# Head rounds of a hybrid attention and mLSTM layer: one quarter of a projection unit goes from slot 0 to slot 14, and three pieces of order with it

## The chip, the cores and the metric

The kernel runs on one core of a Trainium2 chip. The metric is the device time of one execution in microseconds; smaller is better. TensorE (PE) multiplies, PEld is its weight load, VectorE is DVE, ScalarE is ACT, GpSimd is POOL and SyncE is SP.

## The reference

One layer in float32, for 1024 tokens of width 1024. Two mixers read the same normalised input: a differential attention with 8 heads and an mLSTM with 8 heads. Their outputs are gated, projected and added, and a feed-forward part follows.

```python
proj = jnp.einsum('bsd,de->bse', rms_norm(h, norm_mix_w[l]), w_in[l])
(da_q, da_k, da_v, ml_q, ml_k, ml_v, ml_i, ml_f, ml_o, gate_pre) = jnp.split(proj, split_idx, axis=-1)
oa = diff_attention(qa, ka, va, lam, cos, sin)       # softmax(q0 k0) v - lam softmax(q1 k1) v, causal
hm = mlstm_chunkwise(qm, km, vm, i_pre, f_pre)
merged = g[:, :, 0] * (rms_norm(oa) @ w_proj_a) + g[:, :, 1] * ((sigmoid(ml_o) * rms_norm(hm)) @ w_proj_b)
h = h + merged @ w_out
h = h + (relu(rms_norm(h) @ w_ff1) ** 2) @ w_ff2
```

## The kernel before

Products in full precision are made of three matmuls on rounded parts: high times high, high times low, low times high. Each operand is therefore split by one engine into a high part (a copy on ACT) and a low part (a subtraction on DVE or POOL).

The projection of one head is six blocks of 128 columns, and each block is two **units** of 512 tokens. So a head has 12 units, called unit 0 to unit 11 here. Unit k accumulates in the PSUM bank `gp0` if k is even and in `gp1` if it is odd. It has 24 matmuls and is cut into four **quarters** of six. ACT copies a finished bank to `ev0` or `ev1` (the **eviction**, `evac`, L1041), and SP stores it to DRAM. There are only two banks, so on PE a unit begins with a wait (`gp_free`, in `unit`) for the eviction of the unit two before it.

A **head round** works on two heads at once. It makes the 12 units of head h, and between them it does the attention and the mLSTM of head h-1. It has 16 slots. `QUARTERS` gives the number of quarters that PE runs in each slot, and behind them stands the slot's piece of the other head's work, `attend(h, s)`. There are seven head rounds, for h = 1 to 7; a last round of another form (units of the gates, by `GATE_UNITS_AT`) carries the work of head 7.

What `attend` does on PE in the slots that matter: slot 0 transposes v into the banks `tr` and `ob` (L777), slot 2 does the same for the mLSTM's v, slots 3 to 10 make the scores of query tiles 0 to 7 (L799 to L803), slots 4 to 12 transpose the weights of a tile and multiply them by v (L863, L838, L849, L850), slots 11 to 13 hold the mLSTM's products, slot 13 also transposes the attention's output (L890), and slot 15 transposes the mLSTM's output (`hm`, L897), for which DVE must have scaled `nd` (L1625).

Every engine runs its own list in program order. ACT's list for a slot is written by `head_round` in the scalar block: first the split of a weight block into its high part (`split_hi`, L1036) if a block begins in this slot, then the evictions of `ENDS_AT[s][:-1]`, then `attend`, then the eviction of the last unit that ends in this slot. `ENDS_AT[s]` holds the units whose last quarter lies in slot s; it is worked out from `QUARTERS`. In slots 3 to 10 ACT's `attend` ends with the two exponentials of a tile (L1158), which wait for the scores on PE and their maximum on DVE. In slot 0 the eviction stands inside `attend`, behind the copies of k. DVE makes the low parts of k, q and v in slot 0 (L1503 to L1521), the maxima (L1542), the bias `nb` (L1544) and the low parts of the weights (L1526). POOL makes the low parts of the weight blocks (L1910) and one product of the mLSTM in slot 8 (L1934).

Of the kernel before, what the change touches and what calls it, by code (L numbers as in the profile page):

```python
# [26 lines left out]
TT = S // P  # L27
# [52 lines left out]

SLOTS = 16

QUARTERS = (4, 4, 5, 0, 3, 2, 3, 3, 4, 4, 4, 4, 2, 2, 4, 0)


def part_slots(quarters):

    at = [s for s, n in enumerate(quarters) for _ in range(n)]
    starts = [[k for k in range(2 * HB) if at[4 * k] == s] for s in range(SLOTS)]
    ends = [[k for k in range(2 * HB) if at[4 * k + 3] == s] for s in range(SLOTS)]  # L90
    return at, starts, ends


QUARTER_AT, STARTS_AT, ENDS_AT = part_slots(QUARTERS)

# [4 lines left out]
def wait(eng, sem, value):  # L100

    if isinstance(value, int) and value <= 0:
        return
    eng.wait_ge(sem, value)


def tr_index(i, second):

    return i + max(0, i - 4) + (1 if second else 0)
# [22 lines left out]
def build(nc, x, x_rows, positions, norm_mix_w, in_blocks, in_if, columns, da_lambda,  # L132
# [13 lines left out]
    with ExitStack() as ctx:  # L146
        def sb(name, shape, dt=F32, scope=ctx):
            return scope.enter_context(nc.sbuf_tensor(name, shape, dt))
# [69 lines left out]
        with heads, ExitStack() as sc:  # L218
            qraw = sb("qraw", [P, S], F32, sc)
            kraw = sb("kraw", [P, S], F32, sc)  # L220
            qs = sb("qs", [P, 2, S], F32R, sc)
# [809 lines left out]
        def _(act):  # L1031
            def split_hi(n, half_n, slot):

                act.wait_ge(w_loaded[slot], 16 * half_n + 16)
                wait(act, gemm_done, 2 * n - 2)
                act.activation(wh[slot][:], raw[slot][:], ACT.Copy).then_inc(w_hi, 1)  # L1036

            def evac(n, half):
                wait(act, st[half], 16 * n)
                act.wait_ge(gemm_done, 2 * n + half + 1)  # L1040
                act.activation(ev[half][:], gp[half][:], ACT.Copy).then_inc(gp_free, 1)  # L1041
                act.wait_ge(gp_free, 2 * n + half + 1)
                act.sem_inc(ev_ready[half], 1)
# [54 lines left out]
            def units_of_round(h, k):  # L1098
                if k % 2 == 0:
                    b = k // 2  # L1100
                    split_hi(h * HB + b + 1, h * (HB // 2) + (b + 1) // 2, (b + 1) % 2)
# [3 lines left out]
                evac(k // 2, k % 2)  # L1105
                prologue_step(k)

            def attend(h, s, evac_units):
                def v_part(i):
                    act.wait_ge(vtr, 4 * h + 1 + i)  # L1110
                    src = (tr, ob)[i][:].rearrange("p (t n) -> p t n", t=4)
                    act.activation(vs[:, 4 * i:4 * i + 4, 0:DV], src, ACT.Copy).then_inc(v_hi, 1)

                if s == 0:
                    for c, (x_, to) in enumerate(((kraw, ka), (qraw, qs))):
                        act.wait_ge(roped, 2 * h + c + 1)
                        act.activation(to[0:DK, 0, :], x_[0:DK, :], ACT.Copy).then_inc(qk_hi, 1)
                        act.activation(to[DK:P, 1, :], x_[DK:P, :], ACT.Copy).then_inc(qk_hi, 1)
                        if c == 0:
                            act.activation(kb[DK:P, 0, :], x_[0:DK, :], ACT.Copy).then_inc(qk_hi, 1)  # L1120
                            act.activation(kb[0:DK, 1, :], x_[DK:P, :], ACT.Copy).then_inc(qk_hi, 1)
                            evac_units()
                    v_part(0)
                    v_part(1)
                if s == 2:
                    for i in range(2):
                        act.wait_ge(vtr, 4 * h + 3 + i)
# [4 lines left out]
                def high(i, second):  # L1132
                    act.wait_ge(tr_done, 12 * h + tr_index(i, second) + 1)
                    if not second:
                        wait(act, pv_done, TT * h + i)
                    j0, j1 = (4, i + 1) if second else (0, min(4, i + 1))
                    act.activation(ath[:, j0:j1, :], tr[:, 0:(j1 - j0) * P].rearrange("p (j n) -> p j n", n=P),
                                   ACT.Copy).then_inc(a_hi, 1)

                i = s - 5  # L1140
                if 0 <= i < TT:
                    if i >= 4:
                        high(i, True)
                    act.wait_ge(pv_done, TT * h + i + 1)
                    wait(act, sso_done, TT * h + i)
                    act.activation(otmp[:], ob[:, DV:2 * DV], ACT.Copy).then_inc(o_right, 1)
                if 0 <= s - 4 < TT:
                    high(s - 4, False)
                i = s - 5
# [3 lines left out]
                i = s - 3  # L1153
# [44 lines left out]

            def head_round(h, att):
                for s in range(SLOTS):  # L1200
                    for k in STARTS_AT[s]:
                        if k % 2 == 0:
                            units_of_round(h, k)
                    for k in ENDS_AT[s][:-1]:
                        evac(h * HB + k // 2, k % 2)

                    def evac_units():
                        for k in ENDS_AT[s][-1:]:
                            evac(h * HB + k // 2, k % 2)

                    attend(att, s, evac_units)
                    if s:
                        evac_units()

            head_round(1, 0)
            with act.Fori(2, NH) as h:
                head_round(h, h - 1)
            for s in range(SLOTS):
                for k in GATE_UNITS_AT[s]:
                    n = N_GATE + k // 2  # L1220
                    if k % 2 == 0:
                        split_hi(n + 1, (n + 1) // 2, (n + 1) % 2)
                for k in GATE_UNITS_AT[s]:
                    evac(N_GATE + k // 2, k % 2)
                attend(NH - 1, s, lambda: None)
# [17 lines left out]
            for j in range(2 * KT):  # L1243
# [7 lines left out]
                else:  # L1251
                    for i in range(2):
                        k = j - KT
# [151 lines left out]
        def _(dve):  # L1405
# [92 lines left out]
            def attend(h, s):  # L1498
                if s == 0:
                    chain.start(h * DVE_HEAD)  # L1500
                    def low_parts(c, x_, to):
                        dve.wait_ge(qk_hi, 6 * h + 4 * c + 2)
                        dve.tensor_tensor(to[DK:P, 0, :], x_[0:DK, :], to[0:DK, 0, :].bitcast(F32), ALU.subtract).then_inc(qk_lo, 1)  # L1503
                        dve.tensor_tensor(to[0:DK, 1, :], x_[DK:P, :], to[DK:P, 1, :].bitcast(F32), ALU.subtract).then_inc(qk_lo, 1)


                    for x_, turned, s_in in ((kraw, kqs, k_in), (qraw, sg, q_in)):
                        dve.wait_ge(s_in, 16 * 5 * (h + 1))
                        dve.tensor_tensor(turned[:], turned[:], sinT[:], ALU.mult)
                        chain.link(dve.tensor_tensor(x_[:], x_[:], cosT[:], ALU.mult))  # L1510
                        if x_ is qraw:
                            low_parts(0, kraw, ka)
                        dve.tensor_tensor(x_[:], x_[:], turned[:], ALU.add).then_inc(roped, 1)
                    dve.wait_ge(qk_hi, 6 * h + 4)
                    dve.tensor_tensor(kb[0:DK, 0, :], kraw[0:DK, :], kb[DK:P, 0, :].bitcast(F32), ALU.subtract).then_inc(qk_lo, 1)
                    dve.tensor_tensor(kb[DK:P, 1, :], kraw[DK:P, :], kb[0:DK, 1, :].bitcast(F32), ALU.subtract).then_inc(qk_lo, 1)
                    low_parts(1, qraw, qs)
                    for i in range(2):
                        dve.wait_ge(v_hi, 2 * h + i + 1)
                        src = (tr, ob)[i][:].rearrange("p (t n) -> p t n", t=4)  # L1520
                        dve.tensor_tensor(vs[:, 4 * i:4 * i + 4, DV:2 * DV], src, vs[:, 4 * i:4 * i + 4, 0:DV].bitcast(F32),  # L1521
                                          ALU.subtract).then_inc(v_lo, 1)
                def low(i, second):
                    dve.wait_ge(a_hi, 12 * h + tr_index(i, second) + 1)
                    j0, j1 = (4, i + 1) if second else (0, min(4, i + 1))
                    dve.tensor_tensor(atl[:, j0:j1, :], tr[:, 0:(j1 - j0) * P].rearrange("p (j n) -> p j n", n=P),  # L1526
                                      ath[:, j0:j1, :].bitcast(F32), ALU.subtract).then_inc(a_lo, 1)

                i = s - 5
# [6 lines left out]
                if 0 <= s - 4 < TT:  # L1536
                    low(s - 4, False)
                i = s - 3
# [97 lines left out]
            for s in range(SLOTS):  # L1636
                attend(0, s)
            with dve.Fori(1, NH) as h:
                for s in range(SLOTS):
                    attend(h, s)  # L1640
# [5 lines left out]
            for j in range(2 * KT):  # L1646
                n = N_PA + j
                for i in range(2):
                    k = j % KT
# [432 lines left out]
```

## Time and profile before

| | |
|---|---|
| median of 3 runs | 1958.7 us (1956.92 to 1960.9) |
| the profiled execution, its own time | 1959.85 us |
| its span, first to last instruction | 1957.6 us |
| PE busy | 1906.0 us, 97% |
| one head round (526.08 to 630.44 us) | 104.36 us |
| granted TensorE clock, mean | 0.997 |

A view of waits has a row for each pair of an engine's line and the work that released it: total, times, longest. A timeline row is the start, the duration, the engine, the line and the tiles (written from read), and in brackets how long the engine had been idle and what ended that. A PE duration reaches past the start of the next matmul, because they overlap; the distance of two starts is what one costs.

### The profile page before, as it was taken

What the parts mean: (1) busy time and instruction counts of PE and PEld (TensorE: products, weight loads), DVE (VectorE), ACT (ScalarE), POOL (GpSimd) and SP (SyncE); (2) the same over time, 40 slices, a digit from 0 to 9 for tenths busy, and PEclk for the clock granted to TensorE, in tenths of its full rate; (3) what the DMA queues carried; (4) which work ended last, traced back from release to release, by engine and by line L of the source; (5) the groups of instructions that cost most, each with busy time, mean ns of one, the idle gap of its engine ahead of it and who ended that gap; (6) DMA issues with size and microseconds to landing.
All of it is one profiled execution on the core that took longest, in us unless ns stands there. A gap on an engine that the chain in (4) does not pass through costs nothing. (4 is left out here: it accounts for less than half of the span.)

```text
span 1957.6 us, 25826 instructions
## 1 busy us (share of the span) xinstructions
PE 1906.0 (97%) x9314; PEld 1592.5 (81%) x9314; DVE 1188.0 (61%) x1538; ACT 958.3 (49%) x1618; POOL 365.8 (19%) x203
## 2 busy tenths in 40 slices
PE   6999999999999999999999999999999999999998
PEld 5788888888888888878888888878887888888886
DVE  6755666666665757543422122488777777789774
ACT  4355565656564655544434223226485665433341
POOL 1221212112121121212223444440000000121002
PEclk9999999999999999999999999999999999999999
DMA  4251514242423333252244434457576686564412
GB/s 168 89 172 55 178 55 157 74 150 86 148 88 123 107 101 134 72 173 67 81 158 144 156 119 159 174 192 269 201 273 235 211 295 223 187 235 146 155 65 86
DMA packets 91872, 291.77 MB, mean 149 GB/s; under 512 B 10872, under 2 KB 11640, under 8 KB 80784
## 3 DMA queue, kind: packets, MB, share of 16 engines
q1 hardware_dynamic: 89488, 282.31, 41.9%
q10 hardware_dynamic: 2304, 8.39, 1.1%
q8 instruction: 51, 0.84, 0.2%
q14 instruction: 29, 0.24, 0.0%
HBM read 203.56 MB, written 87.10 MB: 148 GB/s over the span
## 5 line engine op out<-in xcount | busy, mean ns | idle before, releaser
L708 PE MATMUL gp<-r1h,w_hi 128*128 128x512 f32 x1152 | 454.6, 395 | 2.2 <-POOL w_lo L1910 2.2
L710 PE MATMUL gp<-r1h,w_lo 128*128 128x512 f32 x1152 | 450.1, 391 | 0.0
L709 PE MATMUL gp<-r1l,w_hi 128*128 128x512 f32 x1152 | 449.5, 390 | 0.0
L1910 POOL TENSOR_TENSOR w_lo<-w_raw,w_hi 128x1024 fp32r<-128x1024 f32 x87 | 218.1, 2507 | 857.3 <-ACT w_hi L1036 857.3
L710 PEld LDWEIGHTS gp<-r1h,w_lo 128*128 128x128 f32 x1152 | 216.6, 188 | 46.4
L708 PEld LDWEIGHTS gp<-r1h,w_hi 128*128 128x128 f32 x1152 | 216.7, 188 | 45.4 <-POOL w_lo L1910 2.6
L709 PEld LDWEIGHTS gp<-r1l,w_hi 128*128 128x128 f32 x1152 | 216.9, 188 | 41.8
L956 PE MATMUL scores<-xh,qh 128*128 128x512 f32 x512 | 200.3, 391 | 3.2 <-ACT res L1309 2.3
L958 PE MATMUL scores<-xl,qh 128*128 128x512 f32 x512 | 199.2, 389 | 0.0
L960 PE MATMUL scores<-xh,ql 128*128 128x512 f32 x512 | 199.2, 389 | 0.0
L1158 ACT ACTIVATE pr<-scores,nb 128x256 f32<-128x256 f32 (+7 forms) x128 | 93.8, 738 | 117.8 <-DVE nb L1544 116.2
L1041 ACT ACTIVATE ev<-gp 128x512 f32<-128x512 f32 x128 | 75.7, 591 | 135.1 <-PE gp L710 129.0
L1722 DVE TENSOR_TENSOR xl<-xraw,xh 128x2048 fp32r<-128x2048 f32 x54 | 132.2, 2447 | 0.0
L1269 ACT ACTIVATE qh<-rq 128x2048 fp32r<-128x2048 f32 x32 | 61.2, 1913 | 117.4 <-DVE rq L1751 71.3
L956 PEld LDWEIGHTS scores<-xh,qh 128*128 128x128 f32 x512 | 96.1, 188 | 25.7 <-ACT res L1309 4.2
L1036 ACT ACTIVATE w_hi<-w_raw 128x1024 fp32r<-128x1024 f32 x88 | 93.0, 1057 | 44.0 <-PE gp L710 21.0
L960 PEld LDWEIGHTS scores<-xh,ql 128*128 128x128 f32 x512 | 96.1, 188 | 20.2
L958 PEld LDWEIGHTS scores<-xl,qh 128*128 128x128 f32 x512 | 96.1, 188 | 20.0 <-issue 0.2
L1542 DVE TENSOR_REDUCE mx<-scores 128x1 f32<-128x256 f32 (+7 forms) x128 | 91.2, 749 | 30.2 <-PE scores L803 29.7
L1281 ACT ACTIVATE xh<-xraw 128x2048 fp32r<-128x2048 f32 x54 | 102.8, 1903 | 9.9 <-DMA xraw<-xo_d 9.8
L1992 POOL TENSOR_TENSOR hb<-hb,sqacc 128x1024 f32<-128x1024 f32 x8 | 24.6, 3074 | 434.4 <-DMA hb<-h_d 434.4
L1726 DVE TENSOR_TENSOR ql<-rq,qh 128x2048 fp32r<-128x2048 f32 x32 | 74.3, 2322 | 46.3 <-ACT qh L1269 46.3
(327 smaller groups left out, 3698.2 us busy)
## 6 DMA issues: line engine op xcount, KB each, us to landing
xraw<-xo_d SPq DMA_DIRECT2D x54, 1024.0 KB, 5.4
w_raw<-in_in_blocks SPq DMA_DIRECT2D x64, 512.0 KB, 3.7
proj_d<-ev SPq DMA_DIRECT2D x128, 256.0 KB, 2.0
rq<-in_ff_quarters SPq DMA_DIRECT2D x32, 1024.0 KB, 8.0
xo_d<-res SPq DMA_DIRECT2D x78, 256.0 KB, 3.3
xo_d<-ring SPq DMA_DIRECT2D x60, 256.0 KB, 3.0
pr<-proj_d SPq DMA_DIRECT2D x16, 512.0 KB, 4.6
gt<-proj_d SPq DMA_DIRECT2D x32, 256.0 KB, 3.5
```

The lines of the kernel that those rows point to most:

```text
L708: pe.matmul(gp[half][:], wh[slot][:, k, :], mh[:, k, t], start=(k == 0), stop=False)
L709: pe.matmul(gp[half][:], wh[slot][:, k, :], ml[:, k, t], start=False, stop=False)
L710: mm = pe.matmul(gp[half][:], wl[slot][:, k, :], mh[:, k, t], start=False, stop=(k == KT - 1))
L956: pe.matmul(bank, qh[s % 3][:, k, cols], xh[s % 3][:, k, :], start=first and k == 0, stop=False, skip_group_check=True)
L958: pe.matmul(bank, qh[s % 3][:, k, cols], xl[s % 3][:, k, :], start=False, stop=False, skip_group_check=True)
L960: mm = pe.matmul(bank, ql[s % 3][:, k, cols], xh[s % 3][:, k, :], start=False, stop=(k == UN - 1), skip_group_check=True)
L1036: act.activation(wh[slot][:], raw[slot][:], ACT.Copy).then_inc(w_hi, 1)
L1158: act.activation(pr[:, c, 0:(i + 1) * P], sp_[:, c, 0:(i + 1) * P], ACT.Exp, bias=nb[:, c:c + 1], scale=SCALE, accum_out=rs[:, i, c:c + 1] ...
L1281: act.activation(xh[s % 3][:], xraw[(s + 1) % 2][:], ACT.Copy).then_inc(p_hi, 1)
L1542: m = dve.tensor_reduce(mx[:, c:c + 1], sp_[:, c, 0:(i + 1) * P], AX_X, ALU.max)
L1722: dve.tensor_tensor(xl[s % 3][:], xraw[(s + 1) % 2][:], xh[s % 3][:].bitcast(F32), ALU.subtract).then_inc(p_lo, 1)
L1910: pool.tensor_tensor(wl[slot][:], raw[slot][:], wh[slot][:].bitcast(F32), ALU.subtract).then_inc(w_split, 1)
```

## The change

`QUARTERS` gives slot 0 three quarters in place of four, and slot 14 five in place of four. As the quarters are dealt to the slots in order, each slot from 1 to 14 that has quarters now begins with the one that had been the last of the slot with quarters before it. `STARTS_AT` and `ENDS_AT` follow from the table. ACT makes the high parts of v ahead of those of q, and DVE the low parts of v ahead of those of q. From slot 9 on ACT splits a weight block behind the copy of the late columns of a tile's weights (`high(i, True)`).

```diff
-QUARTERS = (4, 4, 5, 0, 3, 2, 3, 3, 4, 4, 4, 4, 2, 2, 4, 0)
+QUARTERS = (3, 4, 5, 0, 3, 2, 3, 3, 4, 4, 4, 4, 2, 2, 5, 0)
...
-            def attend(h, s, evac_units):
+            def attend(h, s, evac_units, splits=None):
...
                             evac_units()
-                    v_part(0)
-                    v_part(1)
+                            v_part(0)
+                            v_part(1)
...
                 i = s - 5
+                if 4 <= i < TT:
+                    high(i, True)
+                if splits:
+                    splits()
                 if 0 <= i < TT:
-                    if i >= 4:
-                        high(i, True)
...
-                    for k in STARTS_AT[s]:
-                        if k % 2 == 0:
-                            units_of_round(h, k)
+                    def splits():
+                        for k in STARTS_AT[s]:
+                            if k % 2 == 0:
+                                units_of_round(h, k)
+
+                    if s < 9:
+                        splits()
...
-                    attend(att, s, evac_units)
+                    attend(att, s, evac_units, splits if s >= 9 else None)
...
-                    low_parts(1, qraw, qs)
                     for i in range(2):
                         dve.wait_ge(v_hi, 2 * h + i + 1)
...
+                    low_parts(1, qraw, qs)
```

Worked out from the table, the slot in which each unit ends (and behind whose `attend` it is evicted) is:

| unit | 0 | 1 | 2 | 3 | 4 | 5 | 6 | 7 | 8 | 9 | 10 | 11 |
|---|---|---|---|---|---|---|---|---|---|---|---|---|
| before | 0 | 1 | 2 | 4 | 6 | 7 | 8 | 9 | 10 | 11 | 13 | 14 |
| now | 1 | 2 | 2 | 5 | 6 | 8 | 9 | 10 | 11 | 12 | 14 | 14 |

The first place is PE at the end of slot 8 and the start of slot 9 in the first head round, ahead of unit 7 (bank `gp1`). Before:

```order
L799 MATMUL scores<-mask,identr 128x256
L801 MATMUL scores<-ka,qs 128x256
L803 MATMUL scores<-kb,qs 128x256
L708 MATMUL gp1<-r1h,w_hi1 128x512 [waits gp_free]
L709 MATMUL gp1<-r1l,w_hi1 128x512
L710 MATMUL gp1<-r1h,w_lo1 128x512
```

The same place in the changed kernel:

```order
L799 MATMUL scores<-mask,identr 128x256
L801 MATMUL scores<-ka,qs 128x256
L803 MATMUL scores<-kb,qs 128x256
L708 MATMUL gp0<-r1h,w_hi1 128x512
L709 MATMUL gp0<-r1l,w_hi1 128x512
L710 MATMUL gp0<-r1h,w_lo1 128x512
L708 MATMUL gp0<-r1h,w_hi1 128x512
L709 MATMUL gp0<-r1l,w_hi1 128x512
L710 MATMUL gp0<-r1h,w_lo1 128x512
L708 MATMUL gp1<-r1h,w_hi1 128x512 [waits gp_free]
```

One quarter of unit 6 now stands between the scores of tile 5 and the wait of unit 7.

The second place is ACT from the second sigmoid of slot 7 (`osig`) to the eviction behind the exponentials of tile 5 (`pr`, 128x768) in slot 8. Before:

```order
L1171 ACTIVATE osig<-osig 128x1024 [waits o_in]
L1041 ACTIVATE ev1<-gp1 128x512 [waits gemm_done,proj_stored1]
L1036 ACTIVATE w_hi0<-w_raw0 128x1024 [waits gp_free,gemm_done,w_loaded0]
L1146 ACTIVATE otmp<-ob 128x128 [waits sso_done,pv_done]
L1137 ACTIVATE ath<-tr 128x512 [waits pv_done,tr_done]
L1152 ACTIVATE otmp,sso<-oo 128x128 [waits o_add]
L1158 ACT_TABLE_LOAD [waits a_done]
L1158 ACTIVATE pr,rs<-scores,nb 128x768 [waits nb_ready]
L1158 ACTIVATE pr,rs<-scores,nb 128x768
L1041 ACTIVATE ev0<-gp0 128x512 [waits gemm_done,proj_stored0]
```

In the changed kernel:

```order
L1173 ACTIVATE osig<-osig 128x1024 [waits o_in]
L1036 ACTIVATE w_hi0<-w_raw0 128x1024 [waits gemm_done,w_loaded0]
L1148 ACTIVATE otmp<-ob 128x128 [waits sso_done,pv_done]
L1137 ACTIVATE ath<-tr 128x512 [waits pv_done,tr_done]
L1154 ACTIVATE otmp,sso<-oo 128x128 [waits o_add]
L1160 ACT_TABLE_LOAD [waits a_done]
L1160 ACTIVATE pr,rs<-scores,nb 128x768 [waits nb_ready]
L1160 ACTIVATE pr,rs<-scores,nb 128x768
L1041 ACTIVATE ev1<-gp1 128x512 [waits gemm_done,proj_stored1]
```

The eviction of `gp1` (unit 5), which stood ahead of the split, now stands behind the exponentials.

The third place is ACT in slots 0 to 2 of the first head round, as a piece of the difference:

```order
 L1120 ACTIVATE kb<-kraw 64x1024
 L1121 ACTIVATE kb<-kraw 64x1024
-L1041 ACTIVATE ev0<-gp0 128x512 [waits gemm_done,proj_stored0]
-L1117 ACTIVATE qs<-qraw 64x1024 [waits gp_free,roped]
-L1118 ACTIVATE qs<-qraw 64x1024
 L1112 ACTIVATE vs<-tr 128x4x128 [waits vtr]
 L1112 ACTIVATE vs<-ob 128x4x128 [waits vtr]
-L1041 ACTIVATE ev1<-gp1 128x512 [waits gemm_done,proj_stored1]
+L1117 ACTIVATE qs<-qraw 64x1024 [waits roped]
+L1118 ACTIVATE qs<-qraw 64x1024
+L1041 ACTIVATE ev0<-gp0 128x512 [waits gemm_done,proj_stored0]
 L1036 ACTIVATE w_hi0<-w_raw0 128x1024 [waits gp_free,gemm_done,w_loaded0]
```

The eviction of unit 0 moves from between k and q to behind v and q.

## Rows read from the trace of the kernel before

**Rows 1.** Page: the busy time of each engine.

```profile
PE 1906.0 (97%) x9314; PEld 1592.5 (81%) x9314; DVE 1188.0 (61%) x1538; ACT 958.3 (49%) x1618; POOL 365.8 (19%) x203
```

**Rows 2.** Waits of PE: line, waited for, us in total, times, longest.

```profile
PE tr L897 <- DVE nd L1625: 6.0, 7, 0.9
PE ob L849 <- DVE atl L1526: 3.8, 7, 0.6
PE tr L777 <- DVE vs L1521: 3.2, 6, 0.5
PE scores L882 <- DVE cst L1597: 2.7, 7, 0.4
```

**Rows 3.** Timeline of PE, slots 15 to 2 of one round change.

```profile
526.08 0.66 PE L897 MATMUL tr<-ident,nd 128*128 128x128 f32 x4 [0.87 <-DVE nd L1625]
...
533.28 0.48 PE L708 MATMUL gp<-r1h,w_hi 128*128 128x512 f32 x1
...
546.37 0.66 PE L777 MATMUL tr<-ident,pr 128*128 128x128 f32 x4 [0.54 <-DVE vs L1521]
```

**Rows 4.** Timeline of all engines, the same round, slots 0 and 1.

```profile
538.11 0.57 ACT L1041 ACTIVATE ev<-gp 128x512 f32<-128x512 f32 x1
...
538.73 0.19 PEld L708 LDWEIGHTS gp<-r1h,w_hi 128*128 128x128 f32 x1 [0.16 <-ACT ev L1041]
538.76 1.23 DVE L1513 TENSOR_TENSOR qraw<-qraw,sg 128x1024 f32<-128x1024 f32 x1
...
542.19 0.60 ACT L1112 ACTIVATE vs<-tr 128x512 fp32r<-128x512 f32 x1
```

**Rows 5.** Timeline of PE: first projection matmuls of slots 9 to 12.

```profile
579.18 0.39 PE L708 MATMUL gp<-r1h,w_hi 128*128 128x512 f32 x1
...
580.56 0.39 PE L708 MATMUL gp<-r1h,w_hi 128*128 128x512 f32 x1
...
588.50 0.48 PE L708 MATMUL gp<-r1h,w_hi 128*128 128x512 f32 x1
...
598.97 0.48 PE L708 MATMUL gp<-r1h,w_hi 128*128 128x512 f32 x1
...
609.57 0.48 PE L708 MATMUL gp<-r1h,w_hi 128*128 128x512 f32 x1
```

**Rows 6.** Timeline of ACT: the evictions that close slots 8 to 11.

```profile
585.76 0.59 ACT L1041 ACTIVATE ev<-gp 128x512 f32<-128x512 f32 x1
...
595.42 0.57 ACT L1041 ACTIVATE ev<-gp 128x512 f32<-128x512 f32 x1
...
605.27 0.59 ACT L1041 ACTIVATE ev<-gp 128x512 f32<-128x512 f32 x1
...
610.64 0.59 ACT L1041 ACTIVATE ev<-gp 128x512 f32<-128x512 f32 x1
```

**Rows 7.** Timeline of DVE in slot 8: the bias of tile 5.

```profile
582.23 1.72 DVE L1544 TENSOR_SCALAR nb<-mx 128x2 f32<-128x2 f32 x1
```

**Rows 8.** Timeline of POOL in slot 8.

```profile
581.53 2.39 POOL L1934 TENSOR_TENSOR kqs<-kqs,sg 128x1024 f32<-128x1024 f32 x1
```

**Rows 9.** Timeline of ACT and of PE, slot 0 of the first round.

```profile
120.06 1.06 ACT L1118 ACTIVATE qs<-qraw 64x1024 fp32r<-64x1024 f32 x1
...
116.93 0.48 PE L708 MATMUL gp<-r1h,w_hi 128*128 128x512 f32 x1
```

**Rows 10.** Timeline of PE near the program's start.

```profile
24.60 0.79 PE L734 MATMUL scores<-r1h,wifh 128*128 128x512 f32 x1 [2.60 <-DVE r1l L1426]
...
30.31 0.39 PE L734 MATMUL scores<-r1h,wifh 128*128 128x512 f32 x1
```

**Rows 11.** Timeline of PE, first units of the gates.

```profile
865.18 0.50 PE L708 MATMUL gp<-r1h,w_hi 128*128 128x512 f32 x1 [2.22 <-POOL w_lo L1910]
...
866.76 0.63 PE L708 MATMUL gp<-r1h,w_hi 128*128 128x512 f32 x1
```

**Rows 12.** That stretch: us, five engines' busy time, granted clock, DMA share, GB/s.

```profile
862.00:874.00 12.00, 9.78 (x41) 7.65 (x40) 2.20 (x3) 3.56 (x7) 5.68 (x6) 0.86 0.63 203
```

## The prediction

> **What bounds the kernel now.** I read the page first: PE is busy for 1906.0 us, 97% of the span [rows 1], and no other engine passes 61%. So only what PE waits for can be won or lost, and the waits of PE are the second view. Four rows of it lie in the head rounds: 6.0 us for the scaled `nd` in slot 15, 3.8 us for the low parts of late columns in slot 10, 3.2 us for v's low parts in slot 2, and 2.7 us for the mLSTM's state in slot 13 [rows 2]. That is 15.7 us over seven rounds, all that an edit of these rounds could win from waits. The third view is the timeline of one round, engine beside engine, to see how much time lies between the end of each eviction on ACT and the matmul that needs its bank. There the margin is thin. In slot 0 the eviction of unit 0 starts at 538.11 and takes 0.57 us, and the weight load of unit 2 at 538.73 has already waited 0.16 us for it [rows 4].
>
> **What the change adds: evictions that come too late.** PE has two banks, so unit k+2 waits for the eviction of unit k. Moving one quarter out of slot 0 makes most units end one quarter inside the next slot. Their eviction follows that slot's `attend`, so on ACT it moves back by a whole slot, while on PE the start of unit k+2 moves back by one quarter only. A quarter costs 580.56 - 579.18 = 1.38 us [rows 5]. I take the places in turn, with the round of the rows as the measure; the position of an eviction within its slot is that of the row of before that stood at the same place in ACT's list.
>
> *Slot 9, unit 7 waits for unit 5.* PE is behind the scores of tile 5 at 579.18 and has one quarter to run, until 580.56 [rows 5]. The eviction of unit 5 stood at the end of slot 7, ahead of the split of slot 8; now it stands behind the exponentials of slot 8, where that of unit 6 stood, at 585.76 for 0.59 us [rows 6]. ACT comes there a little sooner: the eviction, 0.57 us, and the wait for its own semaphore no longer stand ahead of the split. The bias of tile 5 took 1.72 us and ended at 583.95, with POOL's product ending at 583.92 beside it [rows 7, 8]; POOL's list follows the split, so both end about 0.75 us sooner. The eviction ends at 585.76 + 0.59 - 0.75 = 585.6. Wait: 5.05 us.
>
> *Slot 10, unit 8 waits for unit 6.* PE: 588.50 + 1.38 = 589.88. ACT: 595.42 + 0.57 = 595.99 [rows 5, 6]. Both shift together, since the exponentials of tile 6 wait for scores that PE makes after its last wait. Wait: 6.1 us.
>
> *Slot 11, unit 9 waits for unit 7.* PE: 598.97 + 1.38 = 600.35. ACT: 605.27 + 0.59 = 605.86 [rows 5, 6]. Wait: 5.5 us.
>
> *Slot 12, unit 10 waits for unit 8.* PE: 609.57 + 1.38 = 610.95; ACT: 610.64 + 0.59 = 611.23 [rows 5, 6]. There are no exponentials in slot 11. Wait: 0.3 us.
>
> *Slot 2, unit 2 waits for unit 0.* The transposes of slot 15 start at 526.08 after a wait of 0.87 us [rows 3]. With one more quarter ahead of them PE comes 1.38 us later: the wait is gone and they start 1.38 - 0.87 = 0.5 us later, and DVE's work behind them too. Behind the transposes of v PE resumes at 533.28 + 0.5 - 1.38 = 532.4 [rows 3], runs five quarters (one of unit 0, four of unit 1), and stands before unit 2 at 539.3. ACT now evicts unit 0 behind v and q. The copies of q wait for q's rotation, which ends at 538.76 + 1.23 + 0.5 = 540.5, so v's copies are done in that time, and the second copy of q gives way where it did, half a microsecond later: 542.19 + 0.5 = 542.7 [rows 4]. The eviction ends at 543.3. Wait: 4.0 us. In the first head round this does not happen: PE resumes at 116.93, stands before unit 2 some 5.5 us later, at 122.4, and the second copy of q is done at 120.06 + 1.06 = 121.1 [rows 9], so the eviction ends at 121.7.
>
> At slots 4 to 8 I cost the change at nothing: unit 3 is evicted behind slot 5 and unit 5 needs its bank only in slot 7; unit 4 stays in slot 6. Two quarters or more and an `attend` cover each. Unit 9's eviction falls behind slot 12, and unit 11 needs it in slot 14. Its store is late on SP and delays the loads of the next k by some 4 us; the rotation that reads them is a slot and more away.
>
> **What it removes.** Of the row for slot 15, 6.0 us, all goes. Of the row for slot 2, 3.2 us, all goes, since PE now reaches slot 2 at 543.3 + 5.5 = 548.8, while DVE is done with v and q half a microsecond later than in the row, at 546.37 + 0.5 = 546.9 [rows 3]. Of the row for slot 10, 3.8 us, all goes: the late columns are copied ahead of the split, and that split is what held them. The row for slot 13 stays, because the chain to it starts in slot 12 behind PE's own work.
>
> **The sum.** For six round changes: 4.0 added, 0.54 and the 0.16 at unit 2 taken away, 3.3 each, 20 us. For seven rounds: 5.05 + 6.1 + 5.5 + 0.3 = 16.95 added and 0.54 taken away, 16.4 each, 115 us. Less the 6.0 us of slot 15. That is 129 us.
>
> **The clock adds to each wait.** PE will stand still 21 times for over 5 us, and six times for 4 us. The trace has one wait of this kind with a fall behind it: PE stood for 2.22 us before 865.18, and from 866.76 on its 128x512 matmuls take 0.63 us in place of 0.39 [rows 11], the levels of 1.2 and 2.4 GHz. The granted clock of these 12 us is 0.86 [rows 12], which is 12 x 0.14 / 0.5 = 3.4 us at the low level, and half of that, 1.7 us, is lost. At the program's start the low level lasted from 24.60, behind 2.60 us of idling, to 30.31 [rows 10]; 5.7 us of work at half rate lose 2.8 us, the dearest case that the trace has. So the cost of one long wait lies between nothing, if a fall happens to end while PE still stands, and 2.8 us. I take 1.6 us for each of the 27, next to the row from the middle of the program: 43 us; the bounds are 0 and 76 us.
> The Trainium skill, TensorE: Matmul & The Clock Gate, "HAM oscillation — how this bites in real kernels", says that an idle stretch between bursts puts the array back to half rate, so that in a loop every burst starts cold, and that the moment varies from run to run. The trace agrees as far as it goes, with 1.7 us at its single case. Left out of the sum, the rule would mean 2088 us in place of 2131.
>
> The profiled execution took 1959.85 us, so its like is 1959.85 + 129 + 43 = 2132. It stood 1.15 us above the median; the predicted median is 2131 us, 172 us slower. About 0.2% is what a measurement of this kernel tells from no change.
>
> **The rivals.**
> *The low level lasts as at the start, behind nearly every wait.* Speaks for it: the waits come four to a round, three of them with some 9 us between, and they are two to three times as long as the two in the rows. Against: the wait of 2.22 us lost 1.7 us only. At 2.8 us each: 1959.85 + 129 + 76 - 1 = 2164; from 2150 up. Chance 0.15.
> *The clock hardly falls.* For it: the fall ends while PE still stands, so that a long wait may cost less than a short one. Against: a wait of 2.22 us was enough. 2088 with no fall at all; up to 2112 here. Chance 0.2.
> *The evictions hold nobody, and the waits that the change aims at go.* The mechanism is that ACT would reach the copy of a bank before PE needs it; it decides if the time from the scores to the end of the exponentials is under one quarter, 1.38 us. The rows say 6 to 7 us (579.18 to 585.76, 588.50 to 595.42) [rows 5, 6], so I see no way but an error in my reading of who waits for which unit. Then six times 0.54, the slot 10 row and half of the slot 15 row go (DVE starts 0.5 us later, which reaches slot 3): some 10 us, 1949. Chance 0.03; some 0.01 for the case that it comes out within 0.2%.
> *The waits are shorter than summed.* If the row positions of ACT are off by 1 us at each of the 27 waits, 27 us less than the forecast: 2104, inside the range.
>
> **How the numbers follow.** Forecast 0.61, with its own range of 2112 to 2150. The range of 8 in 10 takes in about half of either clock rival: 2100 to 2160. Faster 0.03, same 0.01, slower 0.96.
>
> **What would show it.** In the waits of PE a row `gp L708 <- ACT ev L1041` of some 27 long waits, 125 to 145 us in total; PE's busy share down to about 92%; a head round of 124 to 130 us. In a timeline the matmul behind the first quarter of slots 9, 10 and 11 and behind the fifth quarter of slot 2 would be the one with the idle time. Rows `tr L897 <- DVE nd` and `tr L777 <- DVE vs` gone. For the clock: matmuls of 0.63 us behind these waits, and a granted clock of about 0.93 over a round (1.6 us lost at each of four waits is 13 us at the low level). I am wrong if the idle time ahead of L708 is small, or if it sits in other slots than these four, or if the low level holds on through the whole of slots 9 to 12, which would carry the time past 2164.

## The result and the profile after

The changed kernel takes 2137.78 us (median of 4 runs, 2136.72 to 2137.97), the kernel before 1958.62 us in the same session. The ratio is 1.0912, with a 95% interval of 1.0898 to 1.0926: 179.2 us slower. The profiled execution took 2136.72 us.

The page of the kernel after. PE is still the busiest engine, but at 92% and no longer 97% [rows 1]:

```profile
span 2134.9 us, 25826 instructions
PE 1963.2 (92%) x9314; PEld 1632.2 (76%) x9314; DVE 1205.1 (56%) x1538; ACT 956.6 (45%) x1618; POOL 384.6 (18%) x203
core 0: 2134.9 us, clock 0.958
```

PE has the same 9314 matmuls as before and is busy for 57.2 us longer. So about a third of the lost time is slower matmuls, and the granted clock, 0.958 in place of 0.997, says the same. The rest is waiting. The waits of PE after (line, waited for, us in total, times, longest), against [rows 2]:

```profile
PE gp L708 <- ACT ev L1041: 135.2, 28, 6.0
...
PE scores L882 <- DVE cst L1603: 2.7, 7, 0.4
...
PE gp L708 <- POOL w_lo L1916: 0.7, 1, 0.7
```

The first row is new; 27 of its 28 waits are long, and the last is 0.18 us. The rows for `nd`, `atl` and `vs` are gone, 13.0 us together. All waits of PE add up to 161.8 us, against 41.8 before.

The timeline of PE after, in one round and at the round change behind it (start, duration, and in brackets the idle time and what ended it):

```profile
560.79 0.80 PE L708 MATMUL gp<-r1h,w_hi 128*128 128x512 f32 x1 [4.75 <-ACT ev L1041]
...
577.45 0.80 PE L708 MATMUL gp<-r1h,w_hi 128*128 128x512 f32 x1 [5.90 <-ACT ev L1041]
...
594.29 0.80 PE L708 MATMUL gp<-r1h,w_hi 128*128 128x512 f32 x1 [5.30 <-ACT ev L1041]
...
643.50 0.80 PE L708 MATMUL gp<-r1h,w_hi 128*128 128x512 f32 x1 [3.87 <-ACT ev L1041]
644.09 0.63 PE L709 MATMUL gp<-r1l,w_hi 128*128 128x512 f32 x1
...
648.79 0.54 PE L708 MATMUL gp<-r1h,w_hi 128*128 128x512 f32 x1
649.17 0.39 PE L709 MATMUL gp<-r1l,w_hi 128*128 128x512 f32 x1
```

The first three are units 7, 8 and 9, in slots 9, 10 and 11; the fourth is unit 2 in slot 2. Behind the fourth the matmuls take 0.63 us until 648.79, then 0.39 us: the levels of 1.2 and 2.4 GHz.

What PE waited for at 560.79 stands in the timeline of ACT after, in slot 8:

```profile
558.37 0.90 ACT L1160 ACTIVATE pr<-scores,nb 128x768 f32<-128x768 f32 x1 [2.60 <-DVE nb L1550]
...
559.26 0.89 ACT L1160 ACTIVATE pr<-scores,nb 128x768 f32<-128x768 f32 x1
...
560.14 0.59 ACT L1041 ACTIVATE ev<-gp 128x512 f32<-128x512 f32 x1
```

The bank had long been full: PE went on from unit 5 to unit 6 at about 547.4. Its copy of 0.59 us stands behind two exponentials, and these waited 2.60 us for the bias. PE starts 0.06 us behind the copy's end at 560.73.

The windows of after (stretch, us, busy time of PE, PEld, DVE, ACT, POOL, granted clock, DMA share, GB/s). First come one head round and the 8 us from the end of each of its four waits, then the next head round and the 8 us behind its first wait:

```profile
496.63:626.80 130.17, 109.79 (x561) 92.02 (x560) 69.42 (x119) 60.20 (x136) 22.40 (x12) 0.91 0.26 89
...
560.79:568.79 8.00, 8.00 (x34) 6.73 (x35) 1.44 (x3) 0.28 (x1) 0.00 (x0) 0.81 0.33 98
577.45:585.45 8.00, 8.00 (x33) 6.65 (x34) 0.64 (x2) 1.45 (x2) 0.23 (x1) 0.79 0.09 33
594.29:602.29 8.00, 8.00 (x37) 6.75 (x38) 1.97 (x3) 0.49 (x1) 0.00 (x0) 0.77 0.30 98
643.50:651.50 8.00, 8.00 (x24) 6.36 (x25) 5.48 (x4) 1.54 (x2) 4.67 (x5) 0.65 0.44 141
...
626.80:759.40 132.60, 112.26 (x561) 93.71 (x560) 69.40 (x119) 60.18 (x136) 22.40 (x12) 0.90 0.27 90
690.74:698.74 8.00, 8.00 (x26) 6.41 (x27) 1.44 (x3) 0.28 (x1) 0.00 (x0) 0.62 0.33 98
```

A round takes 130.17 us where it took 104.36, and the next one 132.60 us; from the second head round on the two lengths alternate. Their long waits are the same to 0.02 us, so the difference is the clock. The low level is half speed, so a mean of 0.81 over 8 us loses 8 x 0.19 = 1.5 us. The four windows of the first round lose 1.5, 1.7, 1.8 and 2.8 us; behind the first wait of the next round it is 8 x 0.38 = 3.0 us. The same windows behind all 27 long waits lose 1.4 to 3.1 us each, 63 us in all.

### The profile page after: what moved, and what is told of

It is laid out like the page before. It is cut to its first block and busy times, and to the rows that moved or that the text cites. A ratio compares the mean times of both kernels' runs of the same rounds, so it can differ in the third digit from the quotient of the medians.

```text
span 2134.9 us, 25826 instructions
## 1 busy us (share of the span) xinstructions
PE 1963.2 (92%) x9314; PEld 1632.2 (76%) x9314; DVE 1205.1 (56%) x1538; ACT 956.6 (45%) x1618; POOL 384.6 (18%) x203
## 5 line engine op out<-in xcount | busy, mean ns | idle before, releaser
L708 PE MATMUL gp<-r1h,w_hi 128*128 128x512 f32 x1152 | 484.4, 420 | 136.4 <-ACT ev L1041 135.2
L709 PE MATMUL gp<-r1l,w_hi 128*128 128x512 f32 x1152 | 471.9, 410 | 0.0
L710 PE MATMUL gp<-r1h,w_lo 128*128 128x512 f32 x1152 | 469.8, 408 | 0.0
L1916 POOL TENSOR_TENSOR w_lo<-w_raw,w_hi 128x1024 fp32r<-128x1024 f32 x87 | 228.3, 2624 | 1019.4 <-ACT w_hi L1036 1019.4
L708 PEld LDWEIGHTS gp<-r1h,w_hi 128*128 128x128 f32 x1152 | 231.2, 201 | 197.2 <-ACT ev L1041 143.2
L710 PEld LDWEIGHTS gp<-r1h,w_lo 128*128 128x128 f32 x1152 | 230.3, 200 | 51.8
L709 PEld LDWEIGHTS gp<-r1l,w_hi 128*128 128x128 f32 x1152 | 232.1, 201 | 45.5
L1532 DVE TENSOR_TENSOR atl<-tr,ath 128x512 fp32r<-128x512 f32 (+2 forms) x96 | 53.4, 557 | 170.4 <-ACT ath L1137 168.8
L1137 ACT ACTIVATE ath<-tr 128x512 fp32r<-128x512 f32 (+2 forms) x96 | 47.1, 490 | 173.1 <-PE tr L838 156.7
```

What stands on the lines that cost most here:

```text
L708: pe.matmul(gp[half][:], wh[slot][:, k, :], mh[:, k, t], start=(k == 0), stop=False)
L709: pe.matmul(gp[half][:], wh[slot][:, k, :], ml[:, k, t], start=False, stop=False)
L710: mm = pe.matmul(gp[half][:], wl[slot][:, k, :], mh[:, k, t], start=False, stop=(k == KT - 1))
L1916: pool.tensor_tensor(wl[slot][:], raw[slot][:], wh[slot][:].bitcast(F32), ALU.subtract).then_inc(w_split, 1)
```

## The experiments

In early, table_only, filled, late0 and late5 the theory is that of the prediction: evictions that come too late hold PE, and the clock adds to each wait. The rivals differ, and each text names its own. The first four kernels ran beside the kernel before at 1957.67 us, the last four beside it at 1956.97 us.

### early: the evictions go first in their slot

The changed kernel, in which ACT copies a unit whose last quarter is the first of its slot ahead of `attend`, and unit 0 between k and v.

```diff
-for k in ENDS_AT[s][:-1]:
+for k in EARLY_AT[s]:     # last quarter is the first of slot s
     evac(h * HB + k // 2, k % 2)
...
-    for k in ENDS_AT[s][-1:]:
+    for k in LATE_AT[s]:   # the others
```

> The changed kernel with one thing different: a unit whose last quarter is the first of its slot is evicted ahead of that slot's attend (and unit 0 between the copies of k and of v), not behind it. Theory of the late evictions: all 28 waits of PE for ev go, and with them the stretches at the low clock; what is left is DVE's chain to slot 3, 0.25 us a round: 1952 us, 186 us less than the changed kernel. Rival, that the moved quarter itself costs (other waits take over, or PE is slower by its new order): 1990 us or more.

1967.02 us, ratio 1.0047 (1.0034 to 1.0061). The waits of PE in early:

```profile
PE scores L807 <- DVE qs L1518: 18.6, 6, 3.1
...
PE scores L890 <- DVE cst L1611: 2.7, 7, 0.4
```

No wait for an eviction is left, and 170 of the 179 us are back: early is 9 us slower than the kernel before. The late evictions were the main cause. But the kernel is 15 us dearer than expected: a wait of 3.1 us stands at each of six round changes, for the second low part of q, and the granted clock is 0.992. Neither was in the prediction. PE behind one of them, in early:

```profile
552.56 0.58 PE L807 MATMUL scores<-mask,identr 128*128 128x256 f32 x1 [3.09 <-DVE qs L1518]
...
554.00 0.63 PE L716 MATMUL gp<-r1h,w_hi 128*128 128x512 f32 x1
```

### order_only: the old table, the new order

```diff
-QUARTERS = (3, 4, 5, 0, 3, 2, 3, 3, 4, 4, 4, 4, 2, 2, 5, 0)
+QUARTERS = (4, 4, 5, 0, 3, 2, 3, 3, 4, 4, 4, 4, 2, 2, 4, 0)
```

> The changed kernel with the old table of quarters, so only v ahead of q and the splits behind the late columns are left of the change. Theory: these two are harmless and take away the waits of slot 2 (six times 0.54 us) and of slot 10 (seven times 0.53 us), none for evictions: 1951 to 1952 us, 7 us less than before. Rival, that the moved splits or the order of v and q add to the loss: over 1962 us.

1957.37 us, ratio 1.0001 (0.9992 to 1.001): no difference, where a gain of 6 us was expected. The waits of PE in order_only:

```profile
PE scores L799 <- DVE qs L1510: 10.6, 6, 1.8
PE tr L897 <- DVE nd L1631: 5.9, 7, 0.9
```

The waits for `vs` and `atl` went as expected. In their place stands the wait for q once more, 1.8 us each; early's is one quarter (1.38 us) longer, since with the new table PE comes to slot 3 a quarter sooner. To see why, take first the timeline of DVE and of POOL in the kernel before, at the same round change:

```profile
543.78 1.22 DVE L1504 TENSOR_TENSOR qs<-qraw,qs 64x1024 fp32r<-64x1024 f32 x1
545.03 0.69 DVE L1521 TENSOR_TENSOR vs<-tr,vs 128x512 fp32r<-128x512 f32 x1
545.64 0.68 DVE L1521 TENSOR_TENSOR vs<-ob,vs 128x512 fp32r<-128x512 f32 x1
...
545.20 2.37 POOL L1910 TENSOR_TENSOR w_lo<-w_raw,w_hi 128x1024 fp32r<-128x1024 f32 x1 [12.42 <-ACT w_hi L1036]
```

And the same in order_only:

```profile
543.52 1.22 DVE L1509 TENSOR_TENSOR qs<-qraw,qs 64x1024 fp32r<-64x1024 f32 x1
544.76 3.28 DVE L1510 TENSOR_TENSOR qs<-qraw,qs 64x1024 fp32r<-64x1024 f32 x1
...
543.89 3.07 POOL L1916 TENSOR_TENSOR w_lo<-w_raw,w_hi 128x1024 fp32r<-128x1024 f32 x1 [11.44 <-ACT w_hi L1036]
```

Before, v's low parts ran beside POOL's weight split; they read PSUM and took 0.69 and 0.68 us, which is what they also take in order_wait with no work on POOL beside them. With v ahead of q, the second low part of q runs beside it, reads two tiles of SBUF and takes 3.28 us in place of 1.22. It ends at 548.04, and the scores of slot 3 wait for it.

### table_only: the new table, the old order

```diff
-QUARTERS = (4, 4, 5, 0, 3, 2, 3, 3, 4, 4, 4, 4, 2, 2, 4, 0)
+QUARTERS = (3, 4, 5, 0, 3, 2, 3, 3, 4, 4, 4, 4, 2, 2, 5, 0)
```

> The kernel before with the new table of quarters alone. Theory: the table carries the whole loss, through the evictions that it moves by a slot; the wait of slot 10 for the late columns comes on top, half a microsecond in seven rounds: 2141 us (2134 to 2146). Rival, that part of the loss comes from the order of v and q on ACT, which puts unit 0's eviction behind v: 2125 us or less.

2151.48 us, ratio 1.099 (1.0973 to 1.1007), 10 us over what was expected. The table alone makes the kernel slow. The wait at a round change, in the timeline of PE in table_only:

```profile
383.57 0.79 PE L708 MATMUL gp<-r1h,w_hi 128*128 128x512 f32 x1 [4.85 <-ACT ev L1041]
```

It is 4.85 us and not 3.87: the eviction of unit 0 closes the list of slot 1, and there it stands behind q and v, so that v's copies are no longer done while q's rotation runs. The expectation had also added half a microsecond a round for the late columns, and that did not come: table_only has no wait for `atl`, although its splits stand where they stood before, so PE's lateness alone hides it. What has to be explained is then the whole distance between table_only and the kernel after, 13.7 us between the two medians. All waits of PE are 169.9 us against 161.8: 6.2 us more for evictions, nearly all at unit 0, and 1.5 us more ahead of the gates' first unit (2.2 us, as before). The rest, some 5.6 us, is slower matmuls: PE is busy for 1968.2 us against 1963.2. The kernel after gets all this back from its order.

### filled: the waits as after, with PE kept at work

The changed kernel, with matmuls of zero weights into the unit's own bank where PE would stand idle: 20, 25 and 22 at the end of units 6, 7 and 8, and 16 at the end of unit 1 at the six round changes. They add nothing to a sum. Their lengths were chosen to end just short of the eviction.

```diff
+if k == KT - 1:
+    for _ in range(zeros):
+        pe.matmul(gp[half][:], mask[:, 0:P], mh[:, k, t], start=False, stop=False)
```

> The changed kernel, in which PE fills the long waits with matmuls by weights of zero into the bank of the unit at hand: 20, 25 and 22 of them at the end of units 6, 7 and 8 in every head round, and 16 at the end of unit 1 in all rounds but the first. They add nothing to the sums. They are a little shorter than the waits (4.75, 5.9, 5.3, 3.9 us at 0.23 us each), so the evictions come as before, but PE doesn't idle. Theory that some 50 us of the loss are the low clock behind the waits: granted clock back over 0.99, 2085 to 2095 us. Rival, that the rest of the loss is more waiting and not the clock: 2130 us or more, with the clock at 0.99 all the same.

2079.32 us, ratio 1.062 (1.0604 to 1.0636). The page, the waits and the timeline of filled:

```profile
PE 2034.8 (98%) x9879; PEld 1696.6 (82%) x9879; DVE 1205.7 (58%) x1538; ACT 956.8 (46%) x1618; POOL 383.9 (18%) x203
```

```profile
PE gp L711 <- ACT ev L1045: 7.5, 28, 0.3
```

```profile
543.06 5.85 PE L710 MATMUL gp<-r1h,mask 128*128 128x512 f32 x25
549.82 0.50 PE L711 MATMUL gp<-r1h,w_hi 128*128 128x512 f32 x1 [0.23 <-ACT ev L1045]
```

565 matmuls more, and 58.5 us less: 6 us under the range that was expected, since the clock's part is larger than the 50 us assumed. PE does the same useful work and starts each late unit as late as ACT allows, but the granted clock is 0.998. So of the 179.2 us the clock is 58.5, some 2.2 us for each of the 27 long waits, and lateness 120.7. The two kernels were timed in different sessions; against the kernel before in its own session filled is 121.7 us slower, which would leave 57.5 us for the clock. The sum closes from the other side: 565 matmuls at (5.85 - 0.17) / 25 = 0.227 us are 128 us (0.17 us of a duration of 0.39 overlap the next), with the 7.5 us left less the 13.0 us of rows gone 123 us, against the 121.7 measured.

### late0 and late5: one late eviction at a time

late0 is early with unit 0 copied behind v and q, as the kernel after has it. late5 is the kernel before, with unit 5 alone copied behind the exponentials of slot 8.

```diff
-FIRST = [k for k in range(2 * HB) if ... and k not in ()]
+FIRST = [k for k in range(2 * HB) if ... and k not in (0,)]
```

```diff
-for k in ENDS_AT[s][-1:]:
+for k in [] if s == 7 else [5, 6] if s == 8 else ENDS_AT[s][-1:]:
```

> The run with early evictions (1967.0 us) in which unit 0 alone is evicted as in the changed kernel, behind v and q. One wait a round for six rounds, 3.9 us, in front of the one for q's low parts (3.1 us), which it covers. Theory that each wait costs its length and the low clock behind it: 6 x 0.8 for the waiting and some 10 us for the longer stretch at the low level, 1980 to 1984 us. Rival, that the clock's part comes only where waits follow each other closely, as in slots 9 to 11: 1972 us.

> The kernel before with one thing different: unit 5 is evicted behind the exponentials of slot 8 and not behind slot 7. Nothing of the change is in it. Theory: PE stands 6.4 us before unit 7 in each of seven rounds, 45 us, and the clock adds 2.1 us to each (58 us for 28 waits in the changed kernel against the one with filled waits): 2017 us. Rival, that a late eviction costs only together with the moved quarter: under 1970 us.

late0 took 1974.99 us, ratio 1.0095 (1.0079 to 1.011). Its waits of PE:

```profile
PE gp L716 <- ACT ev L1049: 23.2, 6, 3.9
```

The row for q is gone. PE loses 3.9 us ahead of unit 2 and comes to slot 3 so late that q is done. The slot 2 wait of the kernel after thus hides that for q, and what it adds is the 8 us by which late0 exceeds early, not 23. The number of the cheap rival (1972) is nearer than the expectation (1980 to 1984), but its reason is refuted. No other long wait stands near these, and yet the matmuls behind them take 0.63 us, and the 8 us behind each lose 1.5 to 3.0 us, 13.1 us in all. The difference is small because the waits for q in early were paid in the same way: the 8 us behind those six lose 11.2 us.

late5 took 2014.46 us, ratio 1.0294 (1.0278 to 1.031), 57.5 us for seven waits. Its waits of PE:

```profile
PE gp L708 <- ACT ev L1041: 42.7, 7, 6.2
```

One misplaced copy of 0.6 us costs 8.2 us a round: 6.1 of waiting, and 2.1 that are left for the low clock, since nothing else in its waits moved. The granted clock of the 8 us behind its seven waits is 0.69 to 0.73. The rival, that it costs only together with the moved quarter, is refuted.

### order_wait: the split waits for the first low part of q

order_only, in which ACT's weight split of slot 2 waits until DVE has made the first low part of q, so that POOL starts later.

```diff
+if s == 2:
+    act.wait_ge(qk_lo, 6 * att + 5)
 for k in STARTS_AT[s]:
```

> The run with the old table (order_only, 1957.4 us), in which ACT waits for the first low part of q before it splits the weights in slot 2. POOL then makes the low part of the weights behind DVE's work on q and not beside it. Theory that the second low part of q took 3.28 us in place of 1.22 because POOL worked beside it: the wait of slot 3, 1.8 us in six rounds, goes: 1947 us. Rival, that the operation is slow by its own place in the order, or that the later split makes PE or DVE wait in turn: 1957 us or more.

1945.67 us, ratio 0.9938 (0.9925 to 0.9952): 11.3 us faster than before. The timeline of DVE in order_wait, and that of POOL:

```profile
539.72 1.22 DVE L1512 TENSOR_TENSOR qs<-qraw,qs 64x1024 fp32r<-64x1024 f32 x1
...
542.43 1.04 DVE L1552 TENSOR_SCALAR nb<-mx 128x2 f32<-128x2 f32 x1
...
541.04 2.40 POOL L1918 TENSOR_TENSOR w_lo<-w_raw,w_hi 128x1024 fp32r<-128x1024 f32 x1 [13.64 <-ACT w_hi L1036]
```

q's last low part is back at 1.22 us and ends at 540.94, before POOL starts. Nobody waits for q, and the collision was its cause. What collides now is a bias, which takes 1.04 us and holds no one. All waits of PE are 33.0 us against 41.8 before: `vs`, `atl`, and most of the wait of 2.22 us ahead of the gates' first unit [rows 11]. Of that 0.71 us is left, and PE in order_wait goes on at full speed behind it:

```profile
853.67 0.50 PE L708 MATMUL gp<-r1h,w_hi 128*128 128x512 f32 x1 [0.71 <-POOL w_lo L1918]
854.00 0.40 PE L709 MATMUL gp<-r1l,w_hi 128*128 128x512 f32 x1
```

So the 1.7 us that the low level cost there are saved as well. 8.8 and 1.7 are 10.5 of the 11.3 us; the rest is not assigned.

### best: what follows from these

order_wait with the evictions of early and another table; POOL makes its product of slot 8 ahead of that slot's weight split. What each of these is worth was not tried apart.

```diff
-QUARTERS = (4, 4, 5, 0, 3, 2, 3, 3, 4, 4, 4, 4, 2, 2, 4, 0)
+QUARTERS = (4, 4, 5, 0, 3, 2, 3, 3, 3, 4, 4, 4, 2, 2, 5, 0)
```

> The version that the runs point to: v ahead of q and late columns ahead of the split, ACT's wait of order_wait, early evictions, and the quarter for slot 14 taken from slot 8 and not from slot 0, with POOL's product of slot 8 ahead of its low part of the weights. Theory: the waits of slots 15, 2, 3 and 10 are gone, no eviction is late, 6 us less than order_wait: 1941 us. Rival, that slot 8 was as tight as slot 0: waits of PE in slots 8 to 10, 1950 us or more.

1937.45 us, ratio 0.9894 (0.9879 to 0.9909), 1.1% faster than before. A stretch of 103 us in the windows of best (columns as above), and the only wait of its head rounds:

```profile
522.00:625.00 103.00, 102.55 (x569) 87.99 (x568) 67.94 (x121) 61.27 (x136) 20.07 (x12) 1.00 0.33 116
```

```profile
PE scores L890 <- DVE cst L1613: 2.7, 7, 0.4
```

A head round of best takes 101.5 us, by the distance of two such waits (503.77 and 605.30), against 104.36 before. A quarter does move to slot 14 here, but out of slot 8 and not slot 0, and the units that now end on the first quarter of a slot are copied at once. No wait for `nd` is left, the 6 us that the change wanted.

## Why the prediction was right, step by step

**The mechanism** was right: two banks, and copies that come a slot late. table_only shows that the table does it, early that the place of the copies does it, late5 that one late copy does it with nothing else changed.

**The waits.** Predicted 5.05, 6.1 and 5.5 us in slots 9, 10 and 11, and 4.0 in slot 2; measured 4.75, 5.90, 5.30 and 3.87. The reading of who waits for which row was right in all four, each 0.1 to 0.3 us too long. In total 135.2 us, inside 125 to 145. That no long wait stands ahead of unit 2 in the first head round was also right. The head round itself, said to take 124 to 130 us, takes 130.2 or 132.6.

**What goes.** The rows of slots 15, 2 and 10 went, and that of slot 13 stayed, as said. For slot 10 the reason given, the split that no longer stands ahead, is enough by itself (order_only) but was not needed (table_only). Two steps failed without harm to the total. "DVE is done with v and q half a microsecond later than in the row, at 546.37 + 0.5 = 546.9" was wrong; after, q's second low part takes 3.28 us in slot 2:

```profile
645.76 3.28 DVE L1510 TENSOR_TENSOR qs<-qraw,qs 64x1024 fp32r<-64x1024 f32 x1
```

It ends at 649.04, and only PE's own lateness at unit 2 hides it: the scores of slot 3 start at 652.50. I costed the order of v and q at nothing and named no work on POOL beside it. The other step is the wait of 2.22 us ahead of the gates' first unit, which I used as a price for the clock and left out of the sum; 0.7 us is left of it, and order_only, order_wait and early have it so too, while table_only still has 2.2 us: it goes with the order, not with the table.

**The sum of the waits**, 129 us, against 120.0 as the waits of PE go (161.8 - 41.8) and 120.7 as filled has it: 9 us too much: 5.7 us from the 0.1 to 0.3 us at each of 27 waits, 1.5 us from the 2.22 us wait, and some 2 us from slot 12, of which the trace has one wait of 0.18 us in place of seven of 0.3.

**The clock** was the term that was mis-sized: 43 us predicted, 58.5 measured, inside the bounds of 0 and 76. It acts behind each of the 27 long waits. The value taken, 1.6 us each, came from the one row in the middle of the program. Behind the waits of slots 9 to 11 the 8 us windows lose 1.4 to 1.8 us in three rounds, 2.2 to 2.8 us in the first and 2.2 to 3.1 us in the other three; behind the wait of slot 2 they lose 2.8 to 3.0 us. All 27 add up to 63 us, 5 us more than filled gives back; that rest is open. The granted clock of a round was 0.91 or 0.90, not 0.93. Why the rounds alternate no run here shows.

The top price of 2.8 us was also a misreading. The prediction took the low level at the program's start for a fall behind 2.60 us of idling. But four 128x128 transposes at 20.07, ahead of that idling, already take 1.08 us, as four do at 27.32 amid the slow matmuls (1.06 us), where four take 0.66 us in [rows 3]: the clock was low before PE stood, so that stretch says nothing of what a wait costs. That some waits do cost about 2.8 us is luck. The two errors in the sum, 9 us too much and 15 too little, made the total 7 us too low: 2131 against 2137.8.

**The rivals.** That the clock hardly falls (2088 to 2112) is refuted by filled: 58.5 us come back when PE is kept at work. That the low level costs 2.8 us or more is true for ten waits of 27: the six in slot 2, and four in slot 9. That the evictions hold nobody is refuted by the row of 135.2 us.

The Trainium skill, TensorE: Matmul & The Clock Gate, "HAM oscillation — how this bites in real kernels", had every burst behind an idle stretch start cold. The runs agree with it for waits of 3.1 us and more: the clock is down behind every one of them in after, early, late0 and late5. For the waits of 1.77 us in order_only they don't: behind five of six the granted clock stays at 1.00. What such a fall costs is measured, 58.5 us for 27 waits.

## What to carry to other kernels

With two output banks, what counted here is the time from a bank's last matmul to its copy on the other engine's list. A table that moves one quarter must move the copies too, or a copy of 0.6 us can cost 8 us, as in late5. Before an engine's order is changed, look at what runs beside each operation on the engine that it may collide with: v was a harmless neighbour of POOL's split, q was not. A price for idle time on PE has two parts, the wait itself and the slower matmuls behind it, here some 2 us more for 4 to 6 us of waiting.

## What the runs showed of the hardware

**DVE and POOL hold each other up in SBUF.** A subtraction of 64x1024 on DVE takes 1.22 us alone and 3.28 us beside POOL's weight split, whose own 2.40 us become 3.07 to 3.10. After, POOL's split stands at:

```profile
644.87 3.10 POOL L1916 TENSOR_TENSOR w_lo<-w_raw,w_hi 128x1024 fp32r<-128x1024 f32 x1 [11.42 <-ACT w_hi L1036]
```

It ends at 647.97, and DVE's, begun at 645.76, ends 1.07 us behind that, as if it had hardly moved until POOL was through. A bias of 128x2 took 1.67 us in slot 8 of after and 1.72 us before [rows 7], while POOL's product ran beside it, and 0.17 us in the slot behind it, before:

```profile
592.13 0.17 DVE L1544 TENSOR_SCALAR nb<-mx 128x2 f32<-128x2 f32 x1
```

DVE's low parts of v, which have one input in PSUM and one in SBUF, were not held (0.69 and 0.68 us). The Trainium skill, SBUF — State Buffer, "SBUF: two separate sides", says that the two engines share a pair of ports which one instruction holds for its whole length while the other waits, where DVE has two inputs in SBUF and POOL reads SBUF, or where DVE runs in a 2-port mode. The subtraction has two inputs in SBUF, and its durations agree with the page; in which mode the bias, with one tensor as input, ran is shown by no run. An estimate by that rule: POOL's split waits until the first low part of q is done, at 644.51 + 1.22 = 645.73, runs 2.40 us, and the second low part takes 1.22 us behind it, until 649.35. Measured were 649.04. It would have told the prediction to within 0.4 us what the order of v and q costs DVE.

**A short wait need not bring the clock down.** The windows of order_only, the 8 us behind two of its six waits of 1.77 us:

```profile
548.18:556.18 8.00, 8.00 (x41) 6.83 (x42) 3.56 (x12) 3.24 (x13) 0.35 (x3) 1.00 0.60 224
652.77:660.77 8.00, 8.00 (x34) 6.69 (x35) 3.11 (x10) 1.99 (x8) 0.35 (x3) 0.79 0.74 227
```

Behind five of the six the granted clock is 1.00, behind one 0.79. Behind the single wait of 2.22 us in the kernel before it fell [rows 11, 12], and behind the six of 3.1 us in early it is 0.62 to 0.82.

**Idle time is not the cheapest way to wait.** With zero matmuls in the place of the waits, the whole program took 58.5 us less, and the granted clock rose from 0.958 to 0.998.
